# Row sums of a two-block transformer kernel: eight moved to the last second products, the rest out of the joint steps, their rows loaded from GpSimd's queue

## The reference

```python
mod = (jax.nn.silu(c) @ w_ada[l] + b_ada[l])[:, None, :]
sh1, sc1, gt1, sh2, sc2, gt2 = jnp.split(mod, 6, axis=-1)
xn = rms_norm(h, norm1_g[l]) * (1.0 + sc1) + sh1
... # xn @ w_in: attention (MoBA) and a gated recurrence (RWKV-7), mixed, w_out
h = h + gt1 * (mixed @ w_out[l])
xn2 = rms_norm(h, norm2_g[l]) * (1.0 + sc2) + sh2
h = h + gt2 * peer_ffn(xn2, peer_wq[l], peer_subkeys[l], peer_u[l], peer_v[l])
```

## Time and profile before

| | |
|---|---|
| three runs | 1731.22 us median (1730.06 to 1732.92) |
| profiled execution | 1734.15 us, span 1732.3 us |
| TensorE, weight loads | busy 1646.5 us (95%), 1497.3 us |
| VectorE, ScalarE, GpSimd | busy 1135.2, 814.0, 123.4 us |
| mean granted TensorE clock | 0.976 of full speed |
| row sums (line 2274) | 32, median 1218 ns, from 51.3 to 271.6 us |
| remainders on GpSimd (line 2821) | 50, mean 2488 ns |
| DMA | 300.56 MB, mean 174 GB/s |

### The profile page before, as it was taken

How to read it: one execution, slowest core, us unless ns; L and a number is a source line. 1 busy time by engine, 2 the same in 40 slices (tenths; PEclk the granted TensorE clock), 3 DMA queues, 4 the chain that set the end, 5 groups by cost and what they waited for, 6 DMA issues and landing times.

```text
span 1732.3 us, 27151 instructions
## 1 busy us (share of the span) xinstructions
PE 1646.5 (95%) x11430; PEld 1497.3 (86%) x11430; DVE 1135.2 (66%) x1965; ACT 814.0 (47%) x1181; POOL 123.4 (7%) x54
## 2 busy tenths in 40 slices
PE   7999888898999999999999999999999998999998
PEld 4889776798999999998899888888898787999996
DVE  4775675655599789996543576555674464656675
ACT  3644324434444444444444444444434655455663
POOL 0000113200448200000000000000000000000000
PEclk9999898999999999999999999999999998999999
DMA  9534224343454545445565586555655344445331
GB/s 366 222 120 147 74 88 181 122 147 135 160 193 170 195 171 183 158 172 182 190 236 179 189 291 234 193 192 192 262 177 187 121 159 146 168 141 182 125 126 67
DMA packets 48460, 300.56 MB, mean 174 GB/s; under 512 B 5585, under 2 KB 6097, under 8 KB 15826
## 3 DMA queue, kind: packets, MB, share of 16 engines
q1 hardware_dynamic: 43442, 290.28, 47.5%
q10 hardware_dynamic: 4896, 8.54, 1.3%
HBM read 288.18 MB, written 9.44 MB: 172 GB/s over the span
## 4 chain that ended last, share of the span: by engine, by line
PE 86%; DVE 8%; ACT 3%; DMA 1%; issue 1%; POOL 0%; SPq 0%; DVEq 0%; ACTq 0%
PE ps L609 85%; DVE ar L1944 2%; DVE WL L1971 2%; ACT ar L1371 1%; DVE ar L1955 1%; DVE ar L1963 1%; DVE ar L2274 1%; ACT WH L1379 1%; DMA vec<-in_vec 0%; PE ps L790 0%; DMA ar<-in_in_g 0%; DVE ar L2066 0%; ACT X L1843 0%; PE ps L1288 0%; DVE ar L2120 0%
## 5 line engine op out<-in xcount | busy, mean ns | idle before, releaser
L1971 DVE TENSOR_TENSOR WL<-ar,WH 128x1024 fp32r<-128x1024 f32 (+1 forms) x428 | 503.1, 1204 | 342.5 <-ACT WH L1379 341.7
L609 PE MATMUL ps<-RH,WH 128*128 128x256 f32 x2136 | 629.3, 295 | 35.0 <-POOL WL L2821 8.1
L609 PE MATMUL ps<-RH,WL 128*128 128x256 f32 x2136 | 611.2, 286 | 0.0
L609 PE MATMUL ps<-RL,WH 128*128 128x256 f32 x2136 | 611.0, 286 | 0.0
L1379 ACT ACTIVATE WH<-ar 128x1024 fp32r<-128x1024 f32 (+1 forms) x478 | 481.5, 1041 | 275.0 <-PE ps L609 252.5
L609 PEld LDWEIGHTS ps<-RH,WH 128*128 128x128 f32 x2136 | 417.0, 195 | 42.1 <-POOL WL L2821 8.3
L609 PEld LDWEIGHTS ps<-RL,WH 128*128 128x128 f32 x2136 | 416.6, 195 | 2.0 <-issue 1.4
L609 PEld LDWEIGHTS ps<-RH,WL 128*128 128x128 f32 x2136 | 416.1, 195 | 0.0
L609 PE MATMUL ps<-WH,RH 128*128 128x512 f32 (+1 forms) x832 | 325.3, 391 | 7.4 <-DVE RL L2470 4.3
L609 PE MATMUL ps<-WL,RH 128*128 128x512 f32 (+1 forms) x832 | 321.9, 387 | 0.0
L609 PE MATMUL ps<-WH,RL 128*128 128x512 f32 (+1 forms) x832 | 321.7, 387 | 0.0
(11 more groups left out here) (155 smaller groups left out, 943.7 us busy)
## 6 DMA issues: line engine op xcount, KB each, us to landing
ar<-in_u SPq DMA_DIRECT2D x64, 1024.0 KB, 4.9
ar<-in_v SPq DMA_DIRECT2D x64, 1024.0 KB, 4.9
ar<-in_adr SPq DMA_DIRECT2D x16, 1024.0 KB, 5.2
ar<-in_ada SPq DMA_DIRECT2D x8, 1024.0 KB, 12.4
ar<-in_in_g SPq DMA_DIRECT2D x8, 1024.0 KB, 4.9
ar<-in_wq SPq DMA_DIRECT2D x8, 1024.0 KB, 4.9
far_gates<-ar ACTq DMA_DIRECT2D x32, 256.0 KB, 2.0
ar<-far_gates SPq DMA_DIRECT2D x16, 512.0 KB, 4.0
```

What stands on the lines that cost most here:

```text
L609: ins = q.matmul(o, l, r, start=start and i == 0, stop=stop and i == len(pairs) - 1, skip_group_check=skip)
L1971: q.tensor_tensor(l[:, x:z, :], src[:, x:z, :], h[:, x:z, :].bitcast(F32), ALU.subtract).then_inc(*v.up(("lo", n, i)))
```

## The change

`adr` 12 to 15 (eight row sums, columns 40 to 47 of `mod`) leave the front and are summed in `down(3)`, after rounds 1, 3, 5 and 7; their chunks stand in the list behind v 49, 51, 53 and 55. Their slots come from the turning 0, 1, 2. silu(c) is made again: SP loads `cwide` anew in `down(2)` into the room of the far gates, ScalarE takes its sigmoid in round 0 and VectorE multiplies in round 1. The bias of these columns is added after round 7.

In the joint steps of half 1 the sums of `adr` 9 stand in step 0 (before: step 1), and there are no others; `adr` 10 and 11 are summed in steps 2 and 7 of the attention stage (before: half 1 steps 5, 7, 9 and 11 for `adr` 10 to 13, attention steps 0 and 1 for `adr` 14 and 15). `in_g` 3 goes to slot 1 instead of 0, and the later `in_g` chunks alternate between slots 0 and 1.

`adr` 6 to 11 are loaded by GpSimd: when its `Feed` takes `adr` j - 1, it waits for the sums of `adr` j - 1 and issues the load of `adr` j, on a semaphore of its own. The remainders that this `take()` puts into GpSimd's queue stand before.

```diff
-DOTS = ((0, 0, 0, 2, 0, 0, 0, 2, 0, 2, 0, 2), (0, 2, 0, 0, 0, 2) + (0, 2) * 3, (2, 2) + (0,) * 10)
+DOTS = ((0, 0, 0, 2, 0, 0, 0, 2, 0, 2, 0, 2), (2,) + (0,) * 11, (0, 0, 2, 0, 0, 0, 0, 2, 0, 0, 0, 0))
+LATE = (12, 13, 14, 15)
+def late_after(name, b, j):
+    return name == "v" and b == 3 and j in (1, 3, 5, 7)
...
     for n, b in (("u", 0), ("u", 1), ("u", 3), ("v", 1), ("u", 2), ("v", 0), ("v", 2), ("v", 3)):
-        seq += [(n, 16 * b + j) for j in range(16)]
+        for j in range(16):
+            seq += [(n, 16 * b + j)] + ([("adr", LATE[j // 2])] if late_after(n, b, j) else [])
...
+def loaded_by_gpsimd(name, j):
+    return name == "adr" and 6 <= j < LATE[0]
...
     def loaded(self, c):
+        name, j = CHUNKS[c]
+        if loaded_by_gpsimd(name, j):
+            return self.rows_loaded, 16 * (j - 5)
         return self.slot_loaded[chunk_slot(c)], 16 * ROUND[c]
...  # scalar_program, down
+            if b_ == 3 and r == 0:
+                a.wait_ge(m.c_load, 32)
+                AC(m.c_sigmoid_late, m.cwide_late, ACT.Sigmoid, "late c sigmoid")
...
+            if late_after("v", b_, r):
+                feed.take()
...  # vector_program
+    def dots_of(j, silu, need):
+        feed.take()
+        c = CHUNKS.index(("adr", j))
+        w = m.chunk(c)
+        v.wait_ge(*m.loaded(c))
+        for f in range(2):
+            x, i = w[:, 1024 * f:1024 * f + 1024], 16 + 2 * j + f
+            v.wait_ge(*on(need))
+            q.scalar_tensor_tensor(x, x, 1.0, silu, ALU.mult, ALU.mult,
+                                   accum_out=mod[:, i:i + 1]).then_inc(*v.up(("adr", j)))
+            yield
...  # vector_program, down
+            if b_ == 3 and r == 1:
+                v.wait_ge(*on("late c sigmoid"))
+                TT(m.cwide_late, m.cwide_late, m.c_sigmoid_late, ALU.mult, "late c silu")
...
+            if late_after("v", b_, r):
+                finish(dots_of(LATE[r // 2], m.cwide_late, "late c silu"))
+                if r == 7:
+                    TT(mod[:, 40:48], mod[:, 40:48], vc("b_ada", 40, 8), ALU.add)
...  # gpsimd_program
         while feed.taken < c:
+            name, j = CHUNKS[feed.taken]
             feed.take()
+            if loaded_by_gpsimd(name, j + 1):
+                x = CHUNKS.index((name, j + 1))
+                g.wait_ge(*on(("adr", j)))
+                q.dma_start(m.chunk(x), m.D["adr"][j + 1]).then_inc(m.rows_loaded, 16)
...  # sync_program
     for c in dma_order():
         name, j = CHUNKS[c]
+        if loaded_by_gpsimd(name, j):
+            continue
...
+        if (name, j) == ("v", 40):
+            s.wait_ge(*on(("gated", 1)))
+            q.dma_start(m.cwide_late, m.D["cwide"]).then_inc(m.c_load, 16)
```

More of the change, by code:

```diff
@@ L79, in front_order @@
 def front_order():
-    dots = iter([x for j in range(16) for x in (("adr", j), None)])
+    dots = iter([x for j in range(LATE[0]) for x in (("adr", j), None)])
     seq = []
@@ L129, in chunk_slots @@
     slots, n, e = [], 0, 0
-    mixed = range(CHUNKS.index(("in_v", 0)), CHUNKS.index(("adr", 15)) + 1)
+    mixed = range(CHUNKS.index(("in_v", 0)), CHUNKS.index(("adr", LATE[0] - 1)) + 1)
     for c, (name, j) in enumerate(CHUNKS):
@@ L156, in chunk_rounds @@
         s = chunk_slot(c)
-        n[s] += 1
+        n[s] += not loaded_by_gpsimd(*CHUNKS[c])
         rounds.append(n[s])
@@ L171, in dma_order @@
 def dma_order():
-    lo, hi = CHUNKS.index(("in_v", 0)), CHUNKS.index(("adr", 15)) + 1
+    lo, hi = CHUNKS.index(("in_v", 0)), CHUNKS.index(("adr", LATE[0] - 1)) + 1
     split_at = {}
@@ L295, in __init__ @@
         self.slot_loaded = [sem(f"slot{i}_loaded") for i in range(MANY)]
+        self.rows_loaded = sem("rows_loaded")
         self.marks = Marks(self.vec_load)
@@ L412, in peer @@
         self.gate_in = [ar[:, at + 1024 * k:at + 1024 * k + 1024] for k in range(4)]
+        self.cwide_late, self.c_sigmoid_late = self.gate_in[0:2]
         self.HG = [(RH[:, 8 + 2 * i:10 + 2 * i, :], RL[:, 8 + 2 * i:10 + 2 * i, :]) for i in range(2)]
@@ L1123, in dot_chunks @@
     def dot_chunks():
-        for _ in range(16):
+        for _ in range(LATE[0]):
             feed.take()
@@ L2175, in front @@
                 split_act("oms", m.Om, 8)
-        TT(mod[:, 16:48], mod[:, 16:48], vc("b_ada", 16, 32), ALU.add)
+        TT(mod[:, 16:40], mod[:, 16:40], vc("b_ada", 16, 24), ALU.add)
         STT(mod[:, 48:56], mod[:, 32:40], 1.0, vc("n2", 0, 8), ALU.add, ALU.mult)
@@ L2264, in dot_chunks @@
     def dot_chunks():
[L2266 to L2276, removed]
+        for j in range(LATE[0]):
+            yield from dots_of(j, m.cwide, "c wide silu")
+    def dots_of(j, silu, need):
+        feed.take()
+        c = CHUNKS.index(("adr", j))
[7 more added lines that the diff above has]
+            yield
     def queries(i):
@@ L2901, in sync_program @@
     s.wait_ge(m.lora_loads, 80)
-    s.wait_ge(m.c_load, 16)
+    s.wait_ge(m.c_load, 32)
     s.wait_ge(m.table_loads, 48)
```

## The result

The changed kernel takes 1751.32 us (median of 4 runs, 1747.22 to 1755.69), the kernel before, run beside it, 1732.07 (1730.06 to 1733.94): ratio 1.0112, 95% interval 1.0081 to 1.0142, that is 14 to 25 us slower. I had forecast 1738.8, in a range to 1747. The direction was right, the size less than half of it. The profiled execution took 1753.63 us, its span 1751.8.

What follows compares the result with a forecast made beforehand. TensorE, busy 95% of the span, was taken as the bound, so VectorE work counts only where TensorE waits. Terms -7.8 - 10.7 + 6.5 + 19.6 = +7.6 on 1731.22 gave 1738.8 us, range 1731 to 1747.

Steps and rivals of the forecast that it cites:

- Joint step 5: Half 1: without adr 10's row sums the matmuls start 5.47 us earlier and a slow-clock stretch shrinks by 2.3; -7.8 us.
- in_g 3: Its load no longer waits behind adr 15 on SP; the 8.12 us idle and slow clock go, -10.7 us.
- adr 9 in step 0: Half 1: VectorE waits for adr 9's load, q sums start 12.1 us late, some returns; +6.5 us, bounds +3.5 to +11.1.
- adr 10 and 11 in the attention stage: Steps 2 and 7: row sums of 2.30 us each beside full TensorE cost 0.
- The moved remainders: GpSimd's in_g remainders overlap VectorE's products in another place instead: 0, bounds -2 and +2.
- Last second products: v loads wait in SP's order behind adr loads that wait for row sums; +19.6 us, bounds +13.5 to +21.5.
- Rival (c): Front: GpSimd's loads come much later than SP's would; 1743.4 us, some 1747 with adr 10 and 11; chance 0.12.
- (a): Last second products: loads behind adr 12 to 15 are hidden, only the front's -12.0 counts; 1719 us, chance 0.13.
- (b): Front: adr 9 is there when VectorE needs it, or the stall is hidden; 1732.3 us, no change; chance 0.12.
- (d): Front: the stalls do not go because something else, as pm 0, is late; +18 or so, chance 0.03.

Runs made afterwards that it cites:

- A: Changed kernel, but SP issues the loads of adr 13, 14 and 15 two places later, behind the v chunks after each; 1735.23 us, ratio 1.0021.
- D: Changed kernel, but SP loads adr 6 to 11 as before the change; 1750.18 us, ratio 1.0100.
- G: Changed kernel, but adr 12 to 15 in a room of their own outside the turning slots, loaded by GpSimd; 1729.78 us, ratio 0.9977.
- J: I, but the sums of adr 9 in joint step 0; 1724.85 us, ratio 0.9947.
- B: Changed kernel, but the sums of adr 9 back in step 1; 1748.96 us, ratio 1.0091.
- C: Changed kernel with the edits of both A and B; 1731.14 us, ratio 0.9997.
- H: G, but adr 9, 10 and 11 summed in joint steps 7, 9 and 11, none in the attention stage, loaded by SP; 1721.92 us, ratio 0.9934.
- I: H, but in_g 2 to 4 still in slots 0 and 1; 1714.01 us, ratio 0.9894.
- F: Kernel before, with only in_g 3's load issued ahead of adr 14's; 1724.72 us, ratio 0.9950.
- E: Kernel before, with only adr 9's sums moved to joint step 0; 1743.17 us, ratio 1.0050.
- K: Changed kernel run again unchanged, for the second profile; 1753.46 us, ratio 1.0115.

## Why the forecast was too low

I forecast +7.6. The second profile, without its head, has +16.8, and that sum is what I take apart here; the runs' ratio says +19.4 (14 to 25). The 2.6 us between them lie within the interval, and an execution with the slow stretch near 250, like the first profile, adds some 6.

*Joint step 5: right.* -7.8 forecast, -7.9 measured in the six profiles that have this part and adr 9 in step 0 (the changed kernel's two, A, D, G, J). B, C, H and I, with adr 9 elsewhere, have only -4.2 to -5.7 in this stretch: the idle of 5.81 us is gone there too, but each has another slow stretch in it. The idle's share is sure, the clock's (2.3) is not.

*in_g 3: right.* -10.7 forecast, -10.4 measured in every kernel with the stall removed, F among them, where nothing else was changed. That the clock's share is a gain that lasts is less sure: in F 2.7 us were lost at once in the next stretch.

*adr 9 in step 0: mechanism right, term too small.* +6.5 forecast, +9.4 measured, +9.2 alone (E). The load landed nearly as forecast: issued at 177.51 and there 7.57 us later, against 7.0. (In D SP issued it at 178.03, and it was there at the same moment, 185.0.) The q sums start 12.4 us late, for 12.1. The idles of 0.77 and 2.37 us went, and the second slow stretch did not come, as forecast: TensorE's matmuls from the q sums to the product that started at 201.85 before took 19.8 us, and now 17.6 (18.2 in the second profile), 1.6 to 2.2 us less for my 2.5. What failed is the step that took this for a gain in full. Ahead of that product VectorE's chain ends last: it starts when TensorE's work lets it (202.82) and needs 5 us. Before, TensorE was slow beside it and waited 0.37 us for its end; now TensorE is done sooner and stands still 2.05 us at 207.91. E has the same 2.05. So of the 2.9 us by which the term was too small (second profile), 1.7 are this idle, 0.9 clock and 0.3 the later start.

```profile
201.85 2.02 PE L609 MATMUL ps<-ar 128*128 128x128 f32 x16 [0.37 <-DVE ar L1944]
```
```profile
202.82 0.75 DVE L2401 TENSOR_TENSOR ar<-ps,ar 32x256 f32<-32x256 f32 x2 [3.38 <-PE ps L626]
...
206.28 1.49 DVE L1968 TENSOR_TENSOR ar<-ps,con 128x512 f32<-128x512 f32 x2
```

About the load itself, the Trainium skill (SBUF — State Buffer, "SBUF: two separate sides") lets a GpSimd load wait for its descriptors while VectorE runs in a 2-port mode. The trace shows no such cost, but VectorE stood still then: 0.58 us on GpSimd for the issue (SP's in D: 0.43), 7.6 us to landing (SP's in D: 7.0, issued 0.5 later), and D is equal in time.

```profile
177.51 0.58 POOL L2873 DMA_DIRECT2D ar<-in_adr  x1
```

*adr 10 and 11 in the attention stage: wrong.* I wrote "2.30 us each beside full TensorE: 0", and a stretch of 39 us cost +4.0 (3.9 in C, 2.5 in B) in all kernels with the sums there. J, without them, has -0.3. Full TensorE doesn't mean slack in VectorE's chain. VectorE's timeline of the changed kernel shows two places. The sums of adr 10 push the products behind them into GpSimd's remainders (280.69, 5.35 us), where one takes 1.93 us instead of 0.42, and TensorE waits for it at 283.85 (1.28 us); the clock is then low for 3.4 us. The sums of adr 11 do the same at 311: two scalings that take 0.29 and 0.35 us where nothing lies beside them take 2.02 and 2.48, beside remainders from 313.02, and TensorE waits 1.17 us at 318.26. The two idles and the clock's 1.7 are the 4.

```profile
278.94 1.21 DVE L2302 SCALAR_TENSOR_TENSOR ar<-ar 128x1024 f32<-128x1024 f32 x1
...
281.87 1.93 DVE L1968 TENSOR_TENSOR ar<-ar,small 128x256 f32<-128x256 f32 x1
...
315.63 2.48 DVE L2065 TENSOR_SCALAR ar<-ar,small 128x256 f32<-128x256 f32 x1
```
```profile
280.69 5.35 POOL L2856 TENSOR_TENSOR WL<-ar,WH 128x1024 fp32r<-128x1024 f32 x2 [2.02 <-ACT WH L1398]
```
```profile
318.26 0.52 PE L807 MATMUL ps<-con,ar 128*128 128x128 f32 x3 [1.17 <-DVE ar L2065]
```

*The moved remainders: the zero held in the joint steps, by luck.* I took 0 with bounds of 2 for the overlap of GpSimd's remainders. In the changed kernel in_g 1's (178.11 to 182.75) lie beside a VectorE that waits for adr 9. In B they met the row sums, and cost 3.5 us. In the attention stage they are a part of the 4 us above, which I had put at zero.

*Last second products: right.* +19.6 forecast, +21.4 and +21.2 measured. Wait by wait, in the first profile: +6.9 before round 4 (forecast 5.5), then 5.4 and 5.2 (5.3 each), 3.0 at v 58 (2.9), 1.0 behind it (0.6). The excess is in the first: v 52 landed 8.40 us after its issue, where I had 7.1; the later waits go back to trains of 7.2 and 7.02. The clock was low from 1179 to 1186 and 1213 to 1217, and it does add nothing to a pair of rounds: two rounds took 16.24 us (1181.11 to 1197.35) and 16.05, for my 16.2, as the low clock only turns idle into busy time (2.78 us idle and not 5). My count put round 2 at 1158.45, where round 1 starts (v 58, round 10, starts at 1207.28, 5.44 us a round); since only differences enter the sum, this shifts nothing.

*Not in my sum:* +2.0 between 321 and 1147, of which 1.5 is one slow stretch near 790. Nine profiles have it, F among them; before, C, E and I have not, and what decides it stays open. And -1.3 behind the last second products, where before has a slow stretch at 1245 and the changed kernel none.

Summed: 2.9 (adr 9) + 4.0 (attention) + 2.0 (later) + 1.6 (last products) - 1.3 and 0 from the rest = 9.2, all of 16.8 less 7.6. Rival (c) gave a like size for another reason, and D rules it out; (a), (b) and (d) fell. The upper bound of adr 9's term, +11.1, covered what came of it. The terms without a cover were the attention stage's zero and the +2.0: with 6 us between them, they are why the time lies above 1747.

## What to carry to other kernels

Work that fits into an engine's idle time can still cost all of its load's order: ask in which queue and slot its chunk stands, and what stands behind it. Moving one thing in a list shifts all that is scheduled by the list: list the new neighbours of each of them. A stage with TensorE at 100% need not have slack for a VectorE instruction ahead of the product that TensorE waits for next (2.30 us of sums cost 1.28 and 1.17 us of idle here), and a clock that is "given back" counts only if TensorE is what ends last behind it.

## What was not expected of the hardware

- One kernel, the same idle of 1.27 us: in one execution the granted clock was 1.00 from 247 to 252, in another 0.54, and the 28 us to the next mark were 6.1 us longer (first and second profile). Such a stretch near 250 was also in B, C, H and J, and not in A, D, G, I and K: a difference of one of them between two single profiles shows nothing of the kernels.
- The first 176 us took up to 4.2 us less in some executions than in others; F, whose program there is that of before, took 3.9 less.
- Two row sums beside GpSimd's remainders took 5.94 us (B), alone 2.4; a scaling of 128x256 took 2.48 us there, alone 0.35.
